# A hierarchical expert stage: the next expert's gate product between up and down, hidden by one activation ahead of the weight splits, and a plain float down product

## The chip, the cores and the metric

The kernel runs on one core of a Trainium2 chip. The metric is the time of one execution on the device, in microseconds. "Before" is the kernel as it stood; its time is the median of three runs.

## The reference

One step of a one-layer streaming encoder over 304 tokens (16 meta tokens, 256 prompt frames, 32 sample frames) with a model width of 2048, all in float32. A projection feeds an RG-LRU branch and an mLSTM branch, their mix is added to x, and then a hierarchical mixture of experts follows. The change lies in the expert part:

```python
def hier_moe(x, w_rg, b_rg, w_re, b_re, w_g, w_u, w_d):
    ...
    gates = jnp.sum(jax.nn.one_hot(eid, N_EXPERTS, dtype=F32) * top_w[..., None], axis=1)
    for e in range(N_EXPERTS):
        hdn = jax.nn.silu(xf @ w_g[e]) * (xf @ w_u[e])
        out = out + gates[:, e:e + 1] * (hdn @ w_d[e]).astype(F32)
```

There are 16 experts in 4 groups, with w_g and w_u of 2048x512 and w_d of 512x2048. A token goes to one group and to the two best experts in it, so most rows of a dense product would be zero; the kernel gathers the rows of each expert instead.

## The kernel before, in words

The kernel is written by hand for five engines, with semaphores. Up to the router it computes products with 128 weight columns at a time; each float weight and activation is split into a rounded high part (fp32r) and the rounded rest, and three rounded products (high by high, high by low, low by high) stand for one float product. The gate products of the RG-LRU (L639) are plain float products, and so are the transposes and the small sums.

The expert stage starts at L814. Tokens are ranked within their expert; an expert has 64 slots per round, and two experts make a pair of 128 rows. The number of rounds is computed on the chip (`nrounds`) and is 1 with these inputs, so the loop over `nr * NPAIR` runs over eight pairs. POOL gathers the 128 rows of a pair into `rows` (L1764, L1766), and TensorE transposes them into banks 0 to 3 (L825). ScalarE writes their rounded part and VectorE the rest into `xs` (L1131, L1627), side by side, so that one product with a stationary tile of 128 columns takes both: rows 0 to 63 of the result belong to the high part, rows 64 to 127 to the rest, and the two halves are added later.

An expert's weights come as six units of 2 MB: two for gate, two for up, two for down. They lie in `ring`, four slots of 2 MB, and SyncE loads unit n+4 into the slot of unit n when TensorE is done with n (`groups_done`, L544). A unit has two halves. ScalarE copies a half, rounded, into one of four buffers `w_high` (L1125), and VectorE overwrites the half in the ring with the rest, `w_low` (L1620).

TensorE takes gate and up of an expert as 16 products each unit (L847 and L848: high and low weights, 512 columns). ScalarE copies the two results into `gu` (L1139), TensorE adds their halves and turns them by products with `add2` (L861), ScalarE takes silu (L1154), and VectorE multiplies by up into `hf`, rounds it and takes its rest (L1646, L1648, L1650). The down product (L878 to L880) has 64 stationary columns, three rounded products for each of 16 tiles, and adds up in banks 0 to 3. VectorE copies them out into `ysb` (L1660), a slice of the tile that the profile names HB, and POOL stores both experts of a pair to `slot_out` (L1775). The transposes of the next pair's rows need the same banks 0 to 3, and stand between up and down of the second expert (L855).

Every engine executes its own list of instructions in order, so the place of a wait in that list decides what stands behind it. The lists in the loop body, before:

- SyncE: the six units of the first expert, then those of the second, in that order, each with its wait.
- TensorE: for each expert gate, gate, up, up, (transposes in the second), adds, down, down.
- ScalarE: splits of the first four units, with the copies of gate and up among them, the split of the first down unit, silu, (row splits), the other down unit and the first unit of the next expert.
- VectorE: rests of four units, the hidden product and its two parts, (rests of rows), rests of the down units, the wait for the down product, the result copies.

In the profile the buffer numbers are left out, `XG` holds `gu`, `sg` and `hf`, and `tri` holds `add2`.

Of the kernel before, what the change touches and what calls it, by code (L numbers as in the profile page):

```python
# [35 lines left out]
def build(nc, A, O):  # L36
# [6 lines left out]
    P = 128  # L43
# [12 lines left out]
    DE = A["w_exp_gate"].shape[3]  # L56
# [40 lines left out]
    with ctx:  # L97
# [80 lines left out]
        nrounds = sb("nrounds", [P, 1], I32)  # L178
# [45 lines left out]
        hs_high = rounded("hs_high", "XG", HALF + UW + 2 * DE + 2 * HC, HC)  # L224
        hs_low = rounded("hs_low", "XG", HALF + UW + 2 * DE + 3 * HC, HC)
# [84 lines left out]

        FIRST = {"xr": 0, "gr": DR, "q": C_Q, "k": C_Q + NH * DQK, "v": C_V, "og": C_OG, "mgr": C_MG}
# [49 lines left out]
        xgt_ready = sem("xgt_ready")  # L361
# [24 lines left out]
        h_steps = sem("h_steps")  # L386
# [85 lines left out]
        def _(sp):  # L472
# [64 lines left out]
            n = sp.value_load(nrounds[0:1, 0:1], min_val=1, max_val=MAXR)  # L537


            def pair(q, turn):  # L540

                for u in range(4, 12):

                    sp.wait_ge(groups_done, turn * 12 + (G_MOE + u - 3))  # L544
                    sp.dma_start(unit_view(u % 4, u % 6), expert_unit(bass.ds(q * 2 + u // 6, 1), u % 6)
                                 ).then_inc(slot_full[u % 4], 16)

            with sp.Fori(0, n * NPAIR - 1) as t:
                pair(t % NPAIR, t)

                for b in range(4):
                    sp.wait_ge(groups_done, t * 12 + (G_MOE + 8 + b + 1))
                    sp.dma_start(unit_view(b, b), expert_unit(bass.ds(((t + 1) % NPAIR) * 2, 1), b)).then_inc(slot_full[b], 16)
            pair(NPAIR - 1, n * NPAIR - 1)

            sp.wait_ge(groups_done, n * (NPAIR * 12) + (G_MOE - 12 + 8 + 1))
            sp.dma_start(unit_view(0, 0), expert_unit(slice(0, 1), 0)).then_inc(slot_full[0], 16)

            for b in range(4):
                wait_apart(sp, rounds_ready, slot_full[b], n * (NPAIR * 3 * 16) + (LOADS_MOE[b] + (1 if b == 0 else 0)) * 16)  # L560
# [3 lines left out]
        def _(pe):  # L564
# [250 lines left out]
            pe.sem_inc(halves_used, 2)  # L815
            pe.wait_ge(rounds_ready, 1)
            nr = pe.value_load(nrounds[0:1, 0:1], min_val=1, max_val=MAXR)
# [10 lines left out]
            gather_transpose(1)  # L828
            with pe.Fori(0, nr * NPAIR) as p:
                for e in range(2):  # L830
                    if e == 0:
                        pe.wait_ge(xgt_ready, p + 1)


                    for u in range(4):
                        ru, c = 6 * e + u, u // 2
                        if u % 2 == 0:

                            pe.wait_ge(gu_copied, p * 4 + (2 * e + c + 1))
                        for f in range(2):  # L840

                            pe.wait_ge(w_rest, p * 24 + (2 * ru + f + 1))
                            w_hi, w_lo = w_high[(2 * ru + f) % 4], half(w_low[ru % 4], f)
                            for k in range(KE):
                                kk = ((u % 2) * 2 + f) * KE + k
                                lhs = xs[:, kk, e, :]
                                pe.matmul(bank[4 + c][:, 0:DE], lhs, w_hi[:, k, :], start=(kk == 0), stop=False)  # L847
                                last = pe.matmul(bank[4 + c][:, 0:DE], lhs, w_lo[:, k, :], start=False, stop=(kk == KD - 1))  # L848
                            if f == 0:
                                last.then_inc(halves_used, 1)  # L850
                        last.then_inc(groups_done, 1)
# [973 lines left out]
```

## Time and profile before

| | |
|---|---|
| median of 3 runs | 2123.28 us (2123.07 to 2130.36) |
| the profiled execution's own time | 2126.67 us |
| its span in the profile | 2125.2 us |
| TensorE busy | 1898.9 us (89%) |
| VectorE busy | 1248.4 us (59%) |
| ScalarE busy | 1001.4 us (47%) |
| moved by DMA | 426.94 MB, mean 201 GB/s |

Busy time of TensorE is modelled from pipelined products, so neighbouring records overlap; how long a product holds the engine is read from the distance between two starts. The clock column of a stretch is the granted TensorE clock as a share of 2.4 GHz; 0.50 is the lower level, 1.2 GHz. Times in the timeline are from the span's start. A releaser in brackets is what ended the engine's idle time.

### The profile page before, as it was taken

How to read it: one execution, taken by the hardware profiler on the slowest of the kernel's cores; microseconds unless marked ns; L12 is line 12 of the kernel's file. 1: busy time of each engine (PE TensorE's matmuls, PEld its weight loads, DVE VectorE, ACT ScalarE, POOL GpSimd, SP SyncE). 2: the span in 40 equal slices, each digit the busy share in tenths (PEclk: the TensorE clock that was granted, in tenths of full speed). 3: DMA queues.
4: the chain of work that ended last, by engine and by line, in shares of the span. 5: the costliest groups of instructions: out<-in, count | busy, mean ns of one | idle time of the engine just before them, and what ended most of it. 6: DMA issues, size and time to landing. Idle time of an engine off the chain costs nothing.

```text
span 2125.2 us, 27688 instructions
## 1 busy us (share of the span) xinstructions
PE 1898.9 (89%) x11579; PEld 1679.6 (79%) x11579; DVE 1248.4 (59%) x1347; ACT 1001.4 (47%) x928; POOL 100.0 (5%) x188
## 2 busy tenths in 40 slices
PE   6999999999999999999999999656888888888860
PEld 5999999999999999999999999644555555556540
DVE  4764553466555556634344544435888888888763
ACT  4334554453344444442333323205767767676741
POOL 3001001000000000000000000010000000000001
PEclk8999999999999999999999999857999989999885
DMA  7655464454444444455566585415899889889854
GB/s 170 159 159 134 128 162 132 117 149 122 127 127 127 127 127 130 129 159 161 155 157 193 155 203 158 189 37 217 346 385 364 350 332 399 347 336 405 326 200 138
DMA packets 379016, 426.94 MB, mean 201 GB/s; under 512 B 13727, under 2 KB 358651, under 8 KB 362265
## 3 DMA queue, kind: packets, MB, share of 16 engines
q1 hardware_dynamic: 369497, 384.24, 55.6%
q0 software_dynamic: 8080, 34.21, 4.7%
q10 hardware_dynamic: 1344, 7.09, 1.2%
q8 instruction: 76, 1.25, 0.3%
q14 instruction: 19, 0.16, 0.0%
HBM read 410.06 MB, written 15.45 MB: 200 GB/s over the span
## 4 chain that ended last, share of the span: by engine, by line
PE 76%; DVE 9%; DMA 8%; issue 4%; ACT 2%; POOL 1%; DVEq 0%; ACTq 0%; POOLq 0%; SPq 0%
PE bank L583 15%; PE bank L585 15%; PE bank L584 15%; DMA ring<-in_w_exp_down 4%; PE bank L878 3%; PE bank L879 3%; DVE w_low L1620 3%; PE bank L880 3%; PE bank L639 3%; PE bank L743 2%; PE bank L745 2%; PE bank L744 2%; PE bank L847 1%; PE bank L848 1%; PE bank L861 1%
## 5 line engine op out<-in xcount | busy, mean ns | idle before, releaser
L1211 DVE TENSOR_TENSOR low<-ring,high 128x2048 fp32r<-128x2048 f32 x172 | 394.1, 2291 | 564.8 <-ACT high L911 564.5
L583 PE MATMUL bank<-x_high,high 128*128 128x304 f32 x2160 | 661.4, 306 | 1.1 <-DVE low L1211 1.1
L585 PE MATMUL bank<-x_high,low 128*128 128x304 f32 x2160 | 652.2, 302 | 0.0
L911 ACT ACTIVATE high<-ring 128x2048 fp32r<-128x2048 f32 x172 | 329.1, 1913 | 543.7 <-DMA ring<-in_w_in 320.9
L584 PE MATMUL bank<-x_low,high 128*128 128x304 f32 x1904 | 572.3, 301 | 0.0
L1620 DVE TENSOR_TENSOR w_low<-ring,w_high 128x2048 fp32r<-128x2048 f32 x194 | 433.5, 2282 | 68.8 <-ACT w_high L1125 67.6
L1125 ACT ACTIVATE w_high<-ring 128x2048 fp32r<-128x2048 f32 x194 | 364.1, 1913 | 144.1 <-PE bank L880 75.9
L583 PEld LDWEIGHTS bank<-x_high,high 128*128 128x128 f32 x2160 | 406.1, 188 | 6.2 <-issue 3.3
L585 PEld LDWEIGHTS bank<-x_high,low 128*128 128x128 f32 x2160 | 406.1, 188 | 0.0
L584 PEld LDWEIGHTS bank<-x_low,high 128*128 128x128 f32 x1904 | 358.6, 188 | 1.4
L847 PE MATMUL bank<-w_high,xs 128*128 128x512 f32 x512 | 212.3, 415 | 27.5 <-DVE w_low L1620 17.6
L848 PE MATMUL bank<-w_low,xs 128*128 128x512 f32 x512 | 202.1, 395 | 0.0
L847 PEld LDWEIGHTS bank<-w_high,xs 128*128 128x128 f32 x512 | 96.9, 189 | 85.6 <-DVE w_low L1620 62.5
L878 PE MATMUL bank<-w_high,hs_high 128*64 128x512 f32 x256 | 114.1, 446 | 49.1 <-DVE xs L1627 34.3
L584 PE MATMUL bank<-hb_rounded,high 128*128 128x304 f32 x512 | 154.8, 302 | 0.0
L879 PE MATMUL bank<-w_high,hs_low 128*64 128x512 f32 x256 | 111.7, 436 | 0.0
L848 PEld LDWEIGHTS bank<-w_low,xs 128*128 128x128 f32 x512 | 97.3, 190 | 18.2
L880 PE MATMUL bank<-w_low,hs_high 128*64 128x512 f32 x256 | 111.2, 434 | 0.0
L878 PEld LDWEIGHTS bank<-w_high,hs_high 128*64 128x64 f32 x256 | 39.2, 153 | 79.4 <-issue 60.9
L584 PEld LDWEIGHTS bank<-hb_rounded,high 128*128 128x128 f32 x512 | 96.2, 188 | 0.0
L583 PE MATMUL bank<-ym_high,high 128*128 128x304 f32 x256 | 77.7, 304 | 0.0
L585 PE MATMUL bank<-ym_high,low 128*128 128x304 f32 x256 | 77.5, 303 | 0.0
(357 smaller groups left out, 2103.5 us busy)
## 6 DMA issues: line engine op xcount, KB each, us to landing
ring<-in_w_in SPq DMA_DIRECT2D x120, 1024.0 KB, 5.6
ring<-in_w_exp_gate SPq DMA_DIRECT2D x33, 2048.0 KB, 10.4
ring<-in_w_exp_up SPq DMA_DIRECT2D x32, 2048.0 KB, 7.4
ring<-in_w_exp_down SPq DMA_DIRECT2D x32, 2048.0 KB, 9.5
ring<-in_w_proj_rnn SPq DMA_DIRECT2D x20, 1024.0 KB, 5.9
ring<-in_w_proj_mlstm SPq DMA_DIRECT2D x16, 1024.0 KB, 5.9
ring<-in_w_out SPq DMA_DIRECT2D x16, 1024.0 KB, 5.9
slot_out<-HB POOLq DMA_DIRECT2D x8, 1024.0 KB, 11.8
```

The source lines that it names most:

```text
L583: pe.matmul(dst, hi[:, k, :], rhs_high(k), start=(k == 0), stop=False)
L584: pe.matmul(dst, hi[:, k, :], rhs_low(k), start=False, stop=False)
L585: last = pe.matmul(dst, lo[:, k, :], rhs_high(k), start=False, stop=(k == KD - 1))
L847: pe.matmul(bank[4 + c][:, 0:DE], lhs, w_hi[:, k, :], start=(kk == 0), stop=False)
L848: last = pe.matmul(bank[4 + c][:, 0:DE], lhs, w_lo[:, k, :], start=False, stop=(kk == KD - 1))
L878: pe.matmul(dst, hh, w_hi[:, b, :], start=(k == 0), stop=False)
L879: pe.matmul(dst, hl, w_hi[:, b, :], start=False, stop=False)
L880: last = pe.matmul(dst, hh, w_lo[:, b, :], start=False, stop=(k == KE - 1))
L911: act.activation(high[n % 4], raw[n % 4], ACT.Copy).then_inc(t_split, 1)
L1125: act.activation(w_high[(2 * ru + c) % 4], half(w_raw[b], c), ACT.Copy).then_inc(w_split, 1)
L1211: v.tensor_tensor(low[n % 4], raw[n % 4], high[n % 4].bitcast(F32), ALU.subtract).then_inc(t_rest, 1)
L1620: v.tensor_tensor(half(w_low[ru % 4], c), half(w_raw[ru % 4], c), w_high[(2 * ru + c) % 4].bitcast(F32), ALU.subtract).then_inc(w_rest, 1)
```

## The change

The down product takes the float weights from the ring as they are loaded, with `hf` as the stationary operand, so down units are neither split nor rounded. The pipeline over experts is shifted: TensorE computes the next expert's first gate unit before the adds of this expert, its second gate unit after them, and then this expert's down. The transposes of the next rows move between the two up units of the second expert. Rows are split expert by expert. Loads follow TensorE's new order. The splits of the very first unit move ahead of the router's exponentials. The last pair is peeled off the loop, so nothing is gathered, transposed or loaded for a pair that doesn't come; `nrounds` gets a second word, the number of pairs less one (`tail`). A function `p(m, c)` gives `tail * m + c` or the loop's register times m, plus c.

```diff
             def unit(t, j, e, k):
+                sp.wait_ge(groups_done, t * 12 + (G_MOE + j - 1))
+                b = (2 + j) % 4
+                sp.dma_start(unit_view(b, k), expert_unit(e, k)).then_inc(slot_full[b], 16)
+            def pair(q, turn, after):
+                first, second = bass.ds(q * 2, 1), bass.ds(q * 2 + 1, 1)
+                unit(turn, 2, second, 0)
+                unit(turn, 3, second, 1)
+                unit(turn, 4, first, 4)
+                unit(turn, 5, first, 5)
+                unit(turn, 6, second, 2)
+                unit(turn, 7, second, 3)
...
+                    unit(turn, 8, after, 0)
+                    unit(turn, 9, after, 1)
+                    unit(turn, 10, second, 4)
+                    unit(turn, 11, second, 5)
+                    unit(turn, 12, after, 2)
+                    unit(turn, 13, after, 3)
...
+            def down(p, s, e):
+                pe.wait_ge(h_act, p(2, e + 2))
+                for u in range(2):
+                    pe.wait_ge(slot_full[(s + u) % 4], p(48, ((s + u) // 4 + LOADS_MOE[0] + 1) * 16))
+                    for c in range(2):
+                        k = 2 * u + c
+                        w = half(w_raw[(s + u) % 4], c)
+                        for b in range(4):
+                            last = pe.matmul(bank[b][0:CAP, 0:DE], hf[:, k * CAP:(k + 1) * CAP], w[:, b, :],
+                                             start=(k == 0), stop=(k == KE - 1))
+                    last.then_inc(groups_done, 1)
+            def pair(p, more):
+                gate_up(p, 2, 2, 0, 2)
+                gate_up(p, 3, 3, 0, 3)
+                pe.wait_ge(gu_copied, p(4, 1))
+                gate_up(p, 4, 4, 1, 0)
+                add_halves(p, 0)
+                gate_up(p, 5, 5, 1, 1)
+                pe.wait_ge(y_out, p(2, 1))
+                down(p, 6, 0)
+                gate_up(p, 8, 6, 1, 2)
+                if more:
+                    pe.wait_ge(y_out, p(2, 2))
+                    gather_transpose(p(1, 2))
+                gate_up(p, 9, 7, 1, 3)
+                if more:
+                    pe.wait_ge(gu_copied, p(4, 3))
+                    pe.wait_ge(xs_ready[0], p(1, 2))
+                    gate_up(p, 10, 8, 0, 0)
+                add_halves(p, 1)
+                if more:
+                    gate_up(p, 11, 9, 0, 1)
+                    pe.wait_ge(xs_ready[1], p(1, 2))
+                    down(p, 12, 1)
+                else:
+                    pe.wait_ge(y_out, p(2, 2))
+                    down(p, 10, 1)
...
             def pair(p, more):
+                split_unit(p, 4, 4)
+                split_half(p, 5, 5, 0)
+                copy_gu(p, 3, 0, 1)
+                split_half(p, 5, 5, 1)
+                silu_of(p, 0)
+                copy_gu(p, 5, 1, 0)
+                split_unit(p, 8, 6)
+                split_unit(p, 9, 7)
+                if more:
+                    split_half(p, 10, 8, 0)
+                    split_rows(p(1, 2), 0)
+                    split_half(p, 10, 8, 1)
+                    split_half(p, 11, 9, 0)
+                copy_gu(p, 9, 1, 1)
+                if more:
+                    split_half(p, 11, 9, 1)
+                    split_rows(p(1, 2), 1)
+                silu_of(p, 1)
+                if more:
+                    copy_gu(p, 11, 0, 0)
+                    split_unit(p, 14, 10)
+                    split_unit(p, 15, 11)
...
+            def hidden(p, e):
+                v.wait_ge(silu_done, p(2, e + 1))
+                v.tensor_tensor(hf, sg, bank[6][:, HC:2 * HC], ALU.mult).then_inc(h_act, 1)
...
+            def pair(p, more):
+                rest_unit(p, 4, 4)
+                rest_unit(p, 5, 5)
+                hidden(p, 0)
+                rest_unit(p, 8, 6)
+                rest_unit(p, 9, 7)
+                results_out(p, 7, 0)
+                if more:
+                    rest_half(p, 10, 8, 0)
+                    rest_of_rows(p, 8, 0)
+                    rest_half(p, 10, 8, 1)
+                    rest_unit(p, 11, 9)
+                    rest_of_rows(p, 8, 1)
+                hidden(p, 1)
+                if more:
+                    rest_unit(p, 14, 10)
+                    rest_unit(p, 15, 11)
+                    results_out(p, 13, 1)
+                else:
+                    results_out(p, 11, 1)
...
```

Units are numbered here in TensorE's order: 2 and 3 are the first expert's up, 4 and 5 the second's gate, 6 and 7 the first's down, 8 and 9 the second's up, 10 and 11 the next pair's gate, 12 and 13 the second's down, 14 and 15 the next pair's up. `gate_up`, `copy_gu`, `add_halves` and `results_out` hold the same instructions as before, and POOL's list is the old one with the last gather left out.

## Rows read from the trace of the kernel before

**Rows 1.** Page, part 4: the chain that ended last, shares by line.

```profile
PE bank L583 15%; PE bank L585 15%; PE bank L584 15%; DMA ring<-in_w_exp_down 4%; PE bank L878 3%; PE bank L879 3%; DVE w_low L1620 3%; PE bank L880 3%; PE bank L639 3%; PE bank L743 2%; PE bank L745 2%; PE bank L744 2%; PE bank L847 1%; PE bank L848 1%; PE bank L861 1%
```

**Rows 2.** Windows: length, busy us of five engines, clock, DMA share, GB/s; whole stage.

```profile
1447.00:2062.10 615.10, 521.41 (x2192) 353.40 (x2192) 507.14 (x340) 435.21 (x292) 18.80 (x23) 0.92 0.85 343
```

**Rows 3.** Chain in order of time: start us, us; first, last transposes; last copies.

```profile
1507.18 1.75 PE bank L825 x16
...
2038.76 1.75 PE bank L825 x16
...
2060.13 1.88 DVE HB L1660 x3
```

**Rows 4.** Timeline of TensorE in one pair: start us, us.

```profile
1657.34 1.91 PE L825 MATMUL bank<-ident,HB 128*128 128x128 f32 x16
...
1665.27 0.68 PE L878 MATMUL bank<-w_high,hs_high 128*64 128x512 f32 x1 [4.29 <-DVE xs L1627]
...
1667.88 0.44 PE L878 MATMUL bank<-w_high,hs_high 128*64 128x512 f32 x1
...
1677.59 0.39 PE L847 MATMUL bank<-w_high,xs 128*128 128x512 f32 x1
...
1680.99 0.39 PE L848 MATMUL bank<-w_low,xs 128*128 128x512 f32 x1
1682.52 0.50 PE L847 MATMUL bank<-w_high,xs 128*128 128x512 f32 x1 [1.14 <-DVE w_low L1620]
...
1699.03 1.97 PE L861 MATMUL bank<-tri,XG 128*128 128x64 f32 x8 [2.55 <-ACT XG L1139]
1702.79 0.68 PE L878 MATMUL bank<-w_high,hs_high 128*64 128x512 f32 x1 [1.79 <-DVE hs_low L1650]
```

**Rows 5.** Page, part 5: weight rests and splits; busy, mean ns, idle before.

```profile
L1620 DVE TENSOR_TENSOR w_low<-ring,w_high 128x2048 fp32r<-128x2048 f32 x194 | 433.5, 2282 | 68.8 <-ACT w_high L1125 67.6
L1125 ACT ACTIVATE w_high<-ring 128x2048 fp32r<-128x2048 f32 x194 | 364.1, 1913 | 144.1 <-PE bank L880 75.9
```

**Rows 6.** Windows of 5 us in one pair, columns as in rows 2.

```profile
1665.00:1670.00 5.00, 4.73 (x16) 2.66 (x17) 4.52 (x3) 2.44 (x3) 0.00 (x0) 0.70 0.15 62
...
1680.00:1685.00 5.00, 3.79 (x16) 2.50 (x15) 5.00 (x4) 3.40 (x2) 0.62 (x1) 1.00 1.02 351
...
1695.00:1700.00 5.00, 2.45 (x16) 2.21 (x14) 3.74 (x2) 4.98 (x4) 0.57 (x1) 0.87 1.01 429
1700.00:1705.00 5.00, 3.21 (x11) 2.01 (x11) 3.64 (x5) 4.24 (x4) 0.99 (x1) 0.50 1.02 436
```

**Rows 7.** Groups by shape: the plain gate products, and the router's products.

```profile
L639 PE MATMUL bank<-XG,HB 128*128 128x307 f32 x208 | 55.7, 421 | 0.0
...
L799 PE MATMUL bank<-wrt,HB 128*128 128x20 f32 x64 | 13.8, 382 | 0.6 <-DVE HB L1543 0.6
```

**Rows 8.** Timeline of TensorE: twenty records of plain gate products in a row.

```profile
179.99 5.33 PE L639 MATMUL bank<-XG,HB 128*128 128x307 f32 x20
```

**Rows 9.** Timeline of TensorE at the start of the stage.

```profile
1447.01 3.68 PE L825 MATMUL bank<-ident,HB 128*128 128x128 f32 x16 [27.61 <-DMA HB<-xn_rows,gidx]
1454.06 0.79 PE L847 MATMUL bank<-w_high,xs 128*128 128x512 f32 x1 [3.38 <-DVE xs L1635]
...
1459.77 0.40 PE L848 MATMUL bank<-w_low,xs 128*128 128x512 f32 x1
```

**Rows 10.** DMA issues at 1672, 1681, 1681 and 1701 us: KB, us to landing.

```profile
ring<-in_w_exp_up SPq DMA_DIRECT2D x1, 2048.0 KB, 7.3
...
ring<-in_w_exp_down SPq DMA_DIRECT2D x1, 2048.0 KB, 12.6
slot_out<-HB POOLq DMA_DIRECT2D x1, 1024.0 KB, 13.1
...
HB<-xn_rows,gidx POOLq DMA_INDIRECT x1, 9.7
```

**Rows 11.** Timeline of VectorE: the result copies of one expert.

```profile
1677.79 2.48 DVE L1660 COPY HB<-bank 64x512 f32<-64x512 f32 x4 [1.28 <-PE bank L880]
```

More of the change, by code:

```diff
@@ L360, in build @@
         rows_t_done = sem("rows_t_done")
-        xgt_ready = sem("xgt_ready")
+        xs_ready = [sem(f"xs_ready{e}") for e in range(2)]
         h_act = sem("h_act")
@@ new lines, in gate_up @@
+            def gate_up(p, s, q, e, u):
+                dst = bank[4 + u // 2][:, 0:DE]
+                for f in range(2):
+                    pe.wait_ge(w_rest, p(16, 2 * q + f + 1))
+                    w_hi, w_lo = w_high[(2 * q + f) % 4], half(w_low[s % 4], f)
+                    for k in range(KE):
+                        kk = ((u % 2) * 2 + f) * KE + k
+                        pe.matmul(dst, xs[:, kk, e, :], w_hi[:, k, :], start=(kk == 0), stop=False)
+                        last = pe.matmul(dst, xs[:, kk, e, :], w_lo[:, k, :], start=False, stop=(kk == KD - 1))
+                    if f == 0:
+                        last.then_inc(halves_used, 1)
+                last.then_inc(groups_done, 1)
@@ L886, in _ @@
+            gather_transpose(1)
+            pe.wait_ge(xs_ready[0], 1)
+            pe.wait_ge(xs_ready[1], 1)
+            gate_up(first, 0, 0, 0, 0)
+            gate_up(first, 1, 1, 0, 1)
+            with pe.Fori(0, tail) as p:
+                pair(lambda m, c: p * m + c, True)
+            pair(lambda m, c: tail * m + c, False)
         @block.scalar
@@ L1161, in _ @@
+            split_unit(first, 1, 1)
+            split_rows(1, 0)
+            split_rows(1, 1)
+            split_unit(first, 2, 2)
+            copy_gu(first, 1, 0, 0)
+            split_unit(first, 3, 3)
+            with act.Fori(0, tail) as p:
+                pair(lambda m, c: p * m + c, True)
+            pair(lambda m, c: tail * m + c, False)
             for i, (t, n) in enumerate(TT):
@@ L1548, in _ @@
             step(v.memset(rk, 0.0))
+            for c in range(2):
+                v.wait_ge(w_split, c + 1)
+                v.tensor_tensor(half(w_low[0], c), half(w_raw[0], c), w_high[c].bitcast(F32), ALU.subtract).then_inc(w_rest, 1)
             v.wait_ge(logits, 1)
@@ new lines, in results_out, with pair @@
+            def results_out(p, s, e):
+                v.wait_ge(groups_done, p(12, G_MOE + s + 1))
+                if e == 0:
+                    v.wait_ge(y_free, p(1, 1))
+                for b in range(4):
+                    last = v.tensor_copy(ysb[0:CAP, e, b * DE:(b + 1) * DE], bank[b][0:CAP, 0:DE])
+                last.then_inc(y_out, 1)
+            def pair(p, more):
+                rest_unit(p, 4, 4)
[15 more added lines that the diff above has]
+                    results_out(p, 13, 1)
+                else:
+                    results_out(p, 11, 1)
@@ L1664, in _ @@
+            rest_unit(first, 1, 1)
+            rest_of_rows(first, 0, 0)
+            rest_of_rows(first, 0, 1)
+            rest_unit(first, 2, 2)
+            rest_unit(first, 3, 3)
+            with v.Fori(0, tail) as p:
+                pair(lambda m, c: p * m + c, True)
+            pair(lambda m, c: tail * m + c, False)
             for i, (t, n) in enumerate(TT):
```

232 lines of the change are left out of this document (79 added, 153 removed).

## The prediction, made before the changed kernel was run

> **What bounds the kernel now.** The chain of waits comes first: its shares by line name TensorE products almost everywhere, with two strangers among the expert lines, the loads of the down weights and the weight rests on VectorE [rows 1]. So the end of the expert stage is set by TensorE, but not by its work alone. The stage runs from the first row transposes at 1447.0 to the end of the last result copies at 2062.0, which is 615.0 us of the 2125.2 us span. In it TensorE counts as busy for 521 us, the granted clock is 0.92 and the transfers have a share of 0.85 [rows 2, 3]. The chain in order of time has the transposes once per pair of experts: eight of them, 1507.18 to 2038.76, so a pair takes 531.6 / 7 = 75.9 us [rows 3].
>
> The timeline of TensorE inside one pair tells where these go. A gate or up unit (16 products) takes 3.6 us at full pace ((1680.99 - 1677.59) / 15 = 0.227 each); a down product of one expert (48) takes 1677.59 - 1665.27 = 12.3 us, of which 2.6 us, to 1667.88, run at half pace; transposes and adds take 1.75 us each. Eight units, two downs without the slow part (11.0 each), one set of transposes and two sets of adds are 29 + 22 + 5.3 = 56.3 us. The other 19.6 us are mostly the waits of 4.29, 2.55, 1.79 and 1.14 us (the last comes once in either expert), 2.6 us for the half pace after two of them, and the twelve halves of units that come at the pace of the VectorE rest (2.28 us) and not at 1.83 [rows 4, 5]. The transfers aren't the bound yet: full stretches move 429 to 436 GB/s, and right after 1665 they nearly stop, since all four ring slots are held [rows 6]. The two queues that would matter next are thus the ring and VectorE.
>
> **The change, part by part.** The down product becomes plain float. Per expert that removes four weight halves from ScalarE (1.91 us) and VectorE (2.28 us) [rows 5], and the cast and low part of hidden from the path to down. It puts 16 plain products in place of 48 rounded ones. What a plain product costs is in the gate products of the RG-LRU, which are plain: 208 records for 104 products, and 20 records of 307 columns begin in (5.33 - 0.42) / 19 = 258 ns each, two clocks per column [rows 7, 8]. 512 columns are then 0.43 us a record and 0.86 us a product; an expert's down takes 13.8 us, 2.8 more than before. Two places of the Trainium skill differ here. In the Trainium skill, "FP8 and Floating Point Precision", TensorE Precision Notes, true FP32 goes through the array four times, which speaks against giving up three rounded products; the trace agrees, with two records of two clocks per column. In the Trainium skill, "Perfetto Trace Analysis", Engine Utilization, FP32_LOW_HIGH halves the output rate; by that alone a down would take 6.9 us, and the two records do not bear it out.
>
> The next expert's gate product goes between up and down, and silu ahead of the splits that wait for weights. The chain adds, silu (0.4), product (0.4) now runs beside a unit of 3.6 us, so of the waits of 4.29, 2.55 and 1.79 us I cost at most 1.3 us per pair. If that unit is late, the chain is late with it and nothing is lost twice.
>
> What is late next follows from the new orders. The ring is four slots in TensorE's own order, and load n+4 is issued when unit n is done. Two down units now hold two slots for 6.9 and 13.8 us, while only two others can load. And on VectorE the result copies of the first expert stand behind both rests of the second expert's second up unit; TensorE's transposes of the next rows wait for these copies, and everything of TensorE stands behind them. That is a new wait with a loop of its own, from transposes to transposes:
> - A, transposes to the end of the second expert's down: transposes 1.75, three units 10.9, adds 1.75, down 13.8 = 28.2 us. TensorE has then idled for some 7 us, and after 27.6 us idle the first transposes took 3.68 us at clock 0.50 [rows 9], while after 4.3 us the half pace lasted 2.6 us of products [rows 4]. I take both, 1.75 + 1.3; the bounds are 0, and 5.7 us of slow products as after the first transposes (1454.06 to 1459.77), 1.55 more. A = 31.2 us.
> - B, from there to the landing of that up unit: its load is the fifth from the one that the end of the down frees. A unit is 2.097 MB, at 430 GB/s 4.9 us, and lands 7.3 us after issue, so 2.4 us are latency [rows 6, 10]. Issue 0.4, latency 2.4, five units 24.5. The store of results and the gather of rows (1.05 MB each) fall into this stretch, since POOL keeps its order. Each costs at least its bytes, 2.4 us. The store costs at most 5.3, by which a load beside it landed later (12.6 against 7.3); I take 4.0, since the rate fell to 351 GB/s there. For the gather, 2.4 to 4.9 (half of its 9.7 us to landing), I take 2.5, since the stretch with it keeps 436 [rows 6, 10]. B = 33.8 us.
> - C, landing to transposes: two halves on ScalarE 3.8, the second rest 2.3, the copies 2.5, and four hand-overs, 0.6 as an estimate [rows 5, 11]. C = 9.2 us.
>
> The sum is 74.3 us against 75.9: the waits are traded for one of 7 to 8 us, plus 5.6 us of extra down.
>
> The two ends of the stage differ. First, weights of units 0 and 1 are split before the rows arrive; the VectorE part lies beside 13.8 us of router products [rows 7]. Rows are split expert by expert, 1.2 us more than the 7.05 us from transposes to first product [rows 9]. From there six units 21.8, half pace 2.9, one wait of 2.1 for a split behind a copy, adds 1.75, down 13.8, a unit 3.6 and 0.5 of hand-overs: 54.7 us, where the old kernel had 60.2. Last, the loop is peeled: no ninth gather, transposes or row split and no spare load. From the last transposes: A 31.2, three units 10.9, adds 1.75, a unit 3.6, waits 1.5, down 13.8, two units with the wait for the last 8.2, copy and adds 3.3, silu and product 1.5, down 13.8, copies 2.9: 92.4 us. Value loads and one VectorE step ahead of the loop are under 0.5 us, and what follows the stage is the same.
>
> 54.7 + 6 x 74.3 + 92.4 = 592.9 us against 615.0: 22 us less. The profiled execution took 2126.67 us, 3.4 over the median of the runs, so I set 2123.28 - 22 = **2101 us**. One microsecond per period is 6 us; break-even lies at a period of 78.0 us. About 0.5%, 10.6 us, is what a measurement of this kernel can tell from no change, which means periods of 76.2 and 79.7 us.
>
> **Rivals.**
> - The new wait doesn't form: POOL's transfers cost their bytes alone and the clock stays up. The period is 74.3 - 1.7 - 3.05 = 69.5 us and the time 2072 us. For it: full stretches beside the gather kept 436 GB/s. Against: the clock fell after each idle of 2.5 us and more [rows 4, 6].
> - It balances out: the half pace lasts 5.7 us of products and the gather takes half of its landing time, +1.55 + 2.4. The period is 78.2 us and the time 2124 us. For it: after the first transposes the pace stayed low for just so long. Against: in the pairs it lasted 2.6 us.
> - Slower: the gather, now in the one stretch where the transfers bound, holds the loads for its whole 9.7 us: +7.2 us, period 81.5, 2144 us. It decides from 6.2 us upward. Before, it ran into a pause of the ring, so its price is hardly shown; the 436 GB/s speak against it.
> - A plain product takes one record at half rate: every down saves 6.9 us, one on each period and on the first stretch and two at the end, so 2101 - 62 = 2039 us. The two records per product speak against it [rows 7]. (It is the reading that the Trainium skill's "Perfetto Trace Analysis", Engine Utilization, would give.)
>
> **How the numbers follow.** Chances: forecast 0.50, no new wait 0.14, balance 0.22, slower 0.12, half rate 0.02. The forecast's own range, 1.7 us either way per period, is 2091 to 2112 us; nine tenths of it are over 0.5% faster. Faster is 0.45 + 0.14 + 0.02 = 0.61, same 0.05 + 0.20 = 0.25, slower 0.12 + 0.02 = 0.14. The range reaches from the no-wait case, 2068, to 2130, and leaves out the slow and the half-rate case and some of the edges.
>
> **What would show it.** Right: 512 plain down records with a pitch of 0.43 us; 128 weight halves on ScalarE where there were 194; no wait of over 1.3 us between adds and down; TensorE idle for 7 to 8 us ahead of each set of transposes, released by VectorE's result copies, with a granted clock near 0.5 behind it; transposes 74 us apart. Wrong: no such idle time, or the copies early and another releaser there; a store or gather that holds the loads for other than 4.0 and 2.5 us; a plain pitch other than 0.43.

## The result, and the profile after

The changed kernel takes 2090.07 us (median of 4 runs, 2085.14 to 2093.76) against 2123.63 us for the kernel before (4 runs): ratio 0.9833, 95% interval 0.9805 to 0.9862 (ratios here and below are taken over all runs and not from the two medians, so they differ slightly from these). The profiled execution took 2093.76 us, with a span of 2092.2 us; like that of before it lies some 3.5 us over its median.

First the window over the expert stage, from the first row transposes to the last result copies, columns as in rows 2:

```profile
1449.70:2029.00 579.30, 525.80 (x1920) 313.10 (x1920) 344.52 (x268) 303.69 (x250) 15.39 (x21) 0.95 0.88 359
```

Against [rows 2] the stage is 35.8 us shorter, while TensorE is busy for 4.4 us more: its idle time fell from 93.7 to 53.5 us. VectorE lost 163 us of work and ScalarE 132 us. The stage begins 2.7 us later, and what follows it takes 63.2 us as before, so the span is 33.0 us shorter.

In the changed kernel L840 are the transposes, L852 and L853 the gate and up products, L864 the adds, L877 the plain down product, L1148 the weight splits, L1683 their rests and L1709 the result copies. The page's chain by line answers to [rows 1]:

```profile
PE bank L598 16%; PE bank L600 15%; PE bank L599 15%; DMA ring<-in_w_exp_up 5%; PE bank L877 5%; PE bank L852 4%; PE bank L853 3%; PE bank L654 3%; DMA ring<-in_w_exp_gate 2%; PE bank L758 2%; PE bank L760 2%; PE bank L759 2%; DVE w_low L1683 2%; ACT w_high L1148 1%; PE bank L840 1%
```

The down weights' loads (4%) are gone from it and the up weights' loads (5%) have come, and the rests on VectorE fell from 3% to 2%. The page's costliest groups name the same engines as [rows 5]:

```profile
L877 PE MATMUL bank<-ring,XG 128*64 128x512 f32 x512 | 224.8, 597 | 1.0 <-DVE XG L1701 1.0
...
L1683 DVE TENSOR_TENSOR w_low<-ring,w_high 128x2048 fp32r<-128x2048 f32 x126 | 283.8, 2287 | 201.7 <-ACT w_high L1148 201.5
...
L1148 ACT ACTIVATE w_high<-ring 128x2048 fp32r<-128x2048 f32 x128 | 240.2, 1915 | 152.5 <-DMA ring<-in_w_exp_up 104.7
...
L840 PE MATMUL bank<-ident,HB 128*128 128x128 f32 x128 | 27.5, 403 | 67.9 <-DVE HB L1709 39.0
```

There are 512 plain down records, and 128 weight splits where there were 194; a split or rest takes as long as before. The line to read is the last one. Transposes waited for nothing in the loop before; now TensorE idles for 39.0 us ahead of them until VectorE's result copies (L1709) are done. The timeline of TensorE shows this once per pair (some rows; start us, us, in brackets the idle time ahead):

```profile
1506.29 1.96 PE L840 MATMUL bank<-ident,HB 128*128 128x128 f32 x16 [1.80 <-DVE HB L1709]
...
1576.77 3.67 PE L840 MATMUL bank<-ident,HB 128*128 128x128 f32 x16 [6.49 <-DVE HB L1709]
...
1648.66 3.67 PE L840 MATMUL bank<-ident,HB 128*128 128x128 f32 x16 [6.48 <-DVE HB L1709]
1651.98 0.71 PE L852 MATMUL bank<-w_high,xs 128*128 128x512 f32 x1
1652.53 0.39 PE L853 MATMUL bank<-w_low,xs 128*128 128x512 f32 x1
...
1659.71 1.89 PE L864 MATMUL bank<-tri,XG 128*128 128x64 f32 x16
...
1665.22 13.95 PE L877 MATMUL bank<-ring,XG 128*64 128x512 f32 x32
...
1935.94 3.53 PE L840 MATMUL bank<-ident,HB 128*128 128x128 f32 x16 [5.90 <-DVE HB L1709]
```

Six periods, 1506.29 to 1935.94, give 71.6 us each, against 75.9 before. No wait stands between adds and down. VectorE in the same period says why the copies are late:

```profile
1707.71 4.49 DVE L1683 TENSOR_TENSOR w_low<-ring,w_high 128x2048 fp32r<-128x2048 f32 x2 [13.54 <-ACT w_high L1148]
1713.23 4.49 DVE L1683 TENSOR_TENSOR w_low<-ring,w_high 128x2048 fp32r<-128x2048 f32 x2 [1.03 <-ACT w_high L1148]
1717.64 2.47 DVE L1709 COPY HB<-bank 64x512 f32<-64x512 f32 x4
```

The copies stand behind the rests of two units. The second pair of rests is unit 9's, whose load ScalarE had awaited until 1711.29. The down product that feeds the copies ended at 1709.91, 7.7 us before they began:

```profile
1695.96 13.95 PE L877 MATMUL bank<-ring,XG 128*64 128x512 f32 x32
```

ScalarE's wait for unit 9, and POOL's list in the same stretch, the store, the index load and the gather:

```profile
1711.29 3.72 ACT L1148 ACTIVATE w_high<-ring 128x2048 fp32r<-128x2048 f32 x2 [1.80 <-DMA ring<-in_w_exp_up]
...
1682.91 0.62 POOL L1855 DMA_DIRECT2D slot_out<-HB  x1 [50.59 <-DVE HB L1709]
1698.17 0.57 POOL L1844 DMA_DIRECT2D gidx<-slot_token  x1 [14.64 <-issue]
1704.49 0.99 POOL L1846 DMA_INDIRECT HB<-xn_rows,gidx  x1 [5.76 <-DMA gidx<-slot_token]
```

The next three windows lie over the transposes of 1648.66, over the idle time ahead of the next pair's transposes, and over the products behind the first. The granted clock is 0.50 over the transposes and 0.72 over the idle time, and the products right behind run at 1.00 again:

```profile
1648.70:1652.40 3.70, 3.70 (x17) 3.70 (x18) 2.02 (x1) 0.03 (x1) 0.00 (x0) 0.50 1.00 425
1715.00:1720.20 5.20, 0.00 (x0) 0.00 (x0) 5.20 (x7) 1.91 (x2) 0.00 (x0) 0.72 0.98 418
1652.40:1665.20 12.80, 12.80 (x64) 10.41 (x63) 9.86 (x12) 8.98 (x13) 0.00 (x0) 1.00 0.76 300
```

### The profile page after: what moved, and what is told of

Its sections match the earlier page's. It is cut to its first block, busy times and chain, and to the rows that moved or that the text cites. A ratio compares the mean times of both kernels' runs of the same rounds, so it can differ in the third digit from the quotient of the medians.

```text
span 2092.2 us, 26760 instructions
## 1 busy us (share of the span) xinstructions
PE 1905.1 (91%) x11307; PEld 1641.0 (78%) x11307; DVE 1090.6 (52%) x1278; ACT 873.4 (42%) x888; POOL 97.1 (5%) x186
## 4 chain that ended last, share of the span: by engine, by line
PE 77%; DMA 10%; DVE 6%; ACT 3%; issue 2%; POOL 1%; DVEq 0%; ACTq 0%; POOLq 0%; SPq 0%
PE bank L598 16%; PE bank L600 15%; PE bank L599 15%; DMA ring<-in_w_exp_up 5%; PE bank L877 5%; PE bank L852 4%; PE bank L853 3%; PE bank L654 3%; DMA ring<-in_w_exp_gate 2%; PE bank L758 2%; PE bank L760 2%; PE bank L759 2%; DVE w_low L1683 2%; ACT w_high L1148 1%; PE bank L840 1%
## 5 line engine op out<-in xcount | busy, mean ns | idle before, releaser
L1683 DVE TENSOR_TENSOR w_low<-ring,w_high 128x2048 fp32r<-128x2048 f32 x126 | 283.8, 2287 | 201.7 <-ACT w_high L1148 201.5
L1148 ACT ACTIVATE w_high<-ring 128x2048 fp32r<-128x2048 f32 x128 | 240.2, 1915 | 152.5 <-DMA ring<-in_w_exp_up 104.7
L877 PE MATMUL bank<-ring,XG 128*64 128x512 f32 x512 | 224.8, 597 | 1.0 <-DVE XG L1701 1.0
L852 PE MATMUL bank<-w_high,xs 128*128 128x512 f32 x512 | 208.3, 407 | 8.8 <-issue 3.9
L853 PE MATMUL bank<-w_low,xs 128*128 128x512 f32 x512 | 201.0, 393 | 0.0
L877 PEld LDWEIGHTS bank<-ring,XG 128*64 128x64 f32 x512 | 69.2, 138 | 148.0 <-issue 147.3
L852 PEld LDWEIGHTS bank<-w_high,xs 128*128 128x128 f32 x512 | 97.6, 191 | 50.2 <-DVE w_low L1683 22.9
L853 PEld LDWEIGHTS bank<-w_low,xs 128*128 128x128 f32 x512 | 97.4, 190 | 18.5
L840 PE MATMUL bank<-ident,HB 128*128 128x128 f32 x128 | 27.5, 403 | 67.9 <-DVE HB L1709 39.0
L840 PEld LDWEIGHTS bank<-ident,HB 128*128 128x128 f32 x128 | 24.6, 215 | 71.0 <-issue 42.0
## 6 DMA issues: line engine op xcount, KB each, us to landing
ring<-in_w_exp_down SPq DMA_DIRECT2D x32, 2048.0 KB, 12.2
```

What stands on the lines that cost most here:

```text
L840: last = pe.transpose(bank[b][:, c * P:(c + 1) * P], rows[:, k * P:(k + 1) * P], ident[:, :])
L852: pe.matmul(dst, xs[:, kk, e, :], w_hi[:, k, :], start=(kk == 0), stop=False)
L853: last = pe.matmul(dst, xs[:, kk, e, :], w_lo[:, k, :], start=False, stop=(kk == KD - 1))
L877: last = pe.matmul(bank[b][0:CAP, 0:DE], hf[:, k * CAP:(k + 1) * CAP], w[:, b, :], start=(k == 0), stop=(k == KE - 1))
L1148: act.activation(w_high[(2 * q + c) % 4], half(w_raw[s % 4], c), ACT.Copy).then_inc(w_split, 1)
L1683: v.tensor_tensor(half(w_low[s % 4], c), half(w_raw[s % 4], c), w_high[(2 * q + c) % 4].bitcast(F32), ALU.subtract).then_inc(w_rest, 1)
```

## The experiments

Theory: the new wait is the copies' place in VectorE's list, and the gain comes from the order, in which silu's place is essential; the plain product alone gains nothing. Each period below is the mean of the six between the second and the eighth set of transposes, unless the text says otherwise. Two profiles of the changed kernel give 71.6 and 71.4 us, two of the order alone 69.6 and 69.7, so a tenth or two of a microsecond tells nothing. Lines with `<-` and three numbers at the end are waits: who waited for whom, us in total, times, longest.

**The copies ahead of the rests.** On VectorE, in the changed kernel:

```diff
                 rest_unit(p, 8, 6)
-                rest_unit(p, 9, 7)
                 results_out(p, 7, 0)
+                rest_unit(p, 9, 7)
```

> Edit: in the changed kernel, VectorE's result copies of the first expert stand ahead of the rests of unit 9 (the second expert's second up unit) and no longer behind them. Theory (the new wait sets the period): TensorE's idle time of 5.6 to 6.9 us ahead of the transposes goes; the copies (2.5 us) and the transposes (1.75, and 1.6 more at half clock) leave the loop, which then runs from the landing of unit 9 through its split and rest straight to its product. Period 71.6 - 5 = 66 to 67 us, with the 12 loads and POOL's two transfers as the next bound (about 64 us); time 2090 - 6 x 5 = about 2060 us. Rival (unit 9 itself is late, and the copies only fill its waiting time): the transposes move ahead, TensorE waits as long for unit 9, period over 70 us, time within 10 us of 2090.

Measured: 2077.26 us (5 runs), ratio 0.9766 (0.9753 to 0.978), period 68.9 us. The wait for the copies is gone and is worth 2.7 us a period, less than expected: the result lies between the theory and the rival. Ahead of some transposes a new releaser stands in its place, in TensorE's timeline and in POOL's:

```profile
1641.40 1.97 PE L840 MATMUL bank<-ident,HB 128*128 128x128 f32 x16 [2.44 <-DMA HB<-xn_rows,gidx]
...
1709.74 1.97 PE L840 MATMUL bank<-ident,HB 128*128 128x128 f32 x16 [3.38 <-DMA HB<-xn_rows,gidx]
```

```profile
1675.55 0.62 POOL L1855 DMA_DIRECT2D slot_out<-HB  x1 [45.36 <-DVE HB L1709]
1690.73 0.57 POOL L1844 DMA_DIRECT2D gidx<-slot_token  x1 [14.56 <-issue]
1697.17 0.99 POOL L1846 DMA_INDIRECT HB<-xn_rows,gidx  x1 [5.88 <-DMA gidx<-slot_token]
```

POOL's list is serial: the store of a pair's results, a wait of 14.6 us until it has landed, the index load, another 5.9 us, and only then the gather of the next rows. In the six periods TensorE waits for it four times, for 7.0 us in all, so it accounts for only part of what was expected and did not come; the transfers' share over them is 0.97. The transposes have also become quick: behind 2.44 and 3.38 us of idle time they take 1.97 us, not 3.67.

**The plain product alone.** The kernel before, in its own order, with the down product taken plain:

```diff
-                                pe.matmul(dst, hh, w_hi[:, b, :], start=(k == 0), stop=False)
-                                pe.matmul(dst, hl, w_hi[:, b, :], start=False, stop=False)
-                                last = pe.matmul(dst, hh, w_lo[:, b, :], start=False, stop=(k == KE - 1))
...
+                                last = pe.matmul(bank[b][0:CAP, 0:DE], hf[:, k * CAP:(k + 1) * CAP], w[:, b, :],
+                                                 start=(k == 0), stop=(k == KE - 1))
...
-                v.tensor_copy(hs_high, hf).then_inc(h_steps, 1)
...
-                    rest_of_weights(p, 6 * e + 5)
```

> Edit: the kernel before, with its order of units, transposes, loads and silu, and only the down product taken as plain float from the ring (no splits or rests of down units, no rounding of hidden). Theory (the gain is in the order): each down takes 2.8 us longer on TensorE and holds its ring slots that much longer, the splits it saves lie beside other work, and the waits between adds and down stay but for the 0.7 us of rounding; period 75.9 us within 1.5 us, time 2115 to 2132 us. Rival (the gain comes from the lighter ScalarE and VectorE): with a third of their splits gone the period falls to 72 us and the time to 2090 to 2105 us.

Measured: 2134.84 us (5 runs), ratio 1.0041 (1.0027 to 1.0054); 9.2 us slower than the 2125.68 us beside it and 3 us above the theory's range; the rival is out. The period is 76.8 us (seven, 1507.49 to 2045.15). Of TensorE's waits in the loop, the one ahead of the down product for the split rows is still there:

```profile
PE bank L877 <- DVE xs L1625: 25.6, 7, 3.7
```

**Silu late.** In the changed kernel, on ScalarE:

```diff
                 split_half(p, 5, 5, 1)
-                silu_of(p, 0)
                 copy_gu(p, 5, 1, 0)
                 split_unit(p, 8, 6)
+                silu_of(p, 0)
                 split_unit(p, 9, 7)
```

> Edit: in the changed kernel, ScalarE's silu of the first expert stands behind the splits of unit 8 (the second expert's first up unit), so it waits for that unit's load. Theory: unit 8 lands 11 to 13 us after silu's sums are ready, so down starts some 15 us later; the end of down, not the landing of unit 9, then releases the copies and the transposes, so the period rises by about 6 to 10 us, to 78 to 82 us, and the time to 2130 to 2150 us. Rival (the place of silu is of no account, since the loop hangs on unit 9): period within 2 us of 71.6, time within 12 us of 2090.

Measured: 2171.09 us (one run), period 80.7 us. The sign is right. The price, 9.1 us a period, is at the upper end, and the time is 21 us over the expected range, because the two ends pay too: the first stretch takes 68.1 us and not 56.6, the tail 105.5 and not 93.0. Silu waits for a load, TensorE waits for silu's product, and while it waits it frees no ring slot:

```profile
PE bank L877 <- DVE XG L1701: 90.0, 6, 16.0
```

So with silu behind these splits, and the gate product in the same new place, the changed kernel is 45 us slower than the kernel before.

**Half of the down product.** The changed kernel with only the first half of each down unit multiplied; the other half of the product is left out:

```diff
-                    for c in range(2):
+                    for c in range(1):
...
-                                             start=(k == 0), stop=(k == KE - 1))
+                                             start=(k == 0), stop=(k == KE - 2))
```

> Edit: the changed kernel with half of the down product left out (the first of two halves of every down unit alone), so a down takes 6.9 us and not 13.8. Theory (the loop from transposes over the second expert's down to the load that it frees): 6.9 us go from each period, which then meets the bound of the transfers, 64 to 66 us; time 2090 - 6 x 6 - 7 - 14 = about 2033 us. Rival (the ring and the transfers already set the period): period 70 us or more, gain at the two ends alone, time 2065 us or more.

Measured: 2068.91 us (one run), period 69.3 us. Of the 14 us that TensorE no longer works per period, 2.3 come back, far from the theory; the time is the rival's, the period 0.7 us below it. The transposes wait here for the gather too, for up to 6.7 us:

```profile
1709.19 3.67 PE L840 MATMUL bank<-ident,HB 128*128 128x128 f32 x16 [6.66 <-DMA HB<-xn_rows,gidx]
```

That made a second theory: POOL's serial list, not the transfers themselves, is the next bound. It needs the gather alone moved, and with the other edits:

```diff
             def store(p, more):
                 if more:
-                    pool.wait_ge(rows_gathered, (p + 1) * 16)
-                    pool.wait_ge(rows_t_done, p + 1)
-                    gather(p + 1, p + 2)
+                    pool.wait_ge(rows_gathered, (p + 2) * 16)
+                    pool.wait_ge(rows_t_done, p + 2)
+                    gather(p + 2, p + 3)
...
             gather(0, 1)
+            pool.wait_ge(rows_gathered, 16)
+            pool.wait_ge(rows_t_done, 1)
+            gather(1, 2)
...
```

**Early copies and early gather** (the label best):

> The early copies of copies_early, and besides on POOL's list the gather of each pair's rows goes out as soon as the pair before it has been transposed, ahead of the wait for the store, one round early (so there is one gather more in all, of rows that nobody reads). Theory: in copies_early and in half_down the transposes wait for a gather that is late because POOL's list is serial: store, its landing (12.6 to 14.6 us), index, its landing (6 us), gather, its landing (14 us). With the gather out some 45 us earlier its wait goes, and the period falls from 68.9 to what the transfers set: 24 MB of weights, a store and a gather, 27.3 MB in all, at the 418 GB/s of the busiest rows is 65.2 us. So 65.2 to 67.5 for the period, 2055 to 2070 for the run. Rival: copies_early moved 394 GB/s at a DMA share of .96, so the transfers set its period already and the wait for the gather is only where that shows: 68.3 or more, within 5 us of 2077.

Measured: 2067.08 us (5 runs), ratio 0.9728 (0.9713 to 0.9743), period 67.5 us, at the upper end of the theory's range and 0.8 below the rival's. No transposes in the loop wait for anything. Over the six periods TensorE idles for 20 us, where it idled for 39 in the changed kernel, and the transfers reach a share of 0.98:

```profile
1503.49:1908.69 405.20, 385.13 (x1442) 225.19 (x1440) 262.15 (x205) 234.21 (x193) 33.37 (x18) 1.00 0.98 404
```

**The early gather alone.** The changed kernel with POOL's edit only:

> The changed kernel with the early gather alone; the result copies stay behind the rests of unit 9. Theory: there the transposes are released by the result copies, and the gather's own time no longer lies in front of the load of unit 9, so the gather is worth little: period 71.6 within 1, time 2084 to 2094. Rival: the gather still takes its 2.5 us out of the stretch from the second expert's first up product to unit 9's landing: period 69.1 or less, 2076 or less.

Measured: 2086.16 us (5 runs), ratio 0.981 (0.9795 to 0.9825), period 70.4 us. The time is in the theory's range, the period at its lower edge: 1.2 us a period lie between the theory's 0 and the rival's 2.5. In time alone the gain isn't clear, since the interval overlaps the changed kernel's. The copies still release the transposes, after 3.9 to 5.1 us of idle time instead of 5.6 to 6.9.

**A second store.** That kernel, with each pair's results stored twice:

```diff
                 pool.dma_start(slot_out[bass.ds(p * P, P), :].rearrange("(e s) n -> s e n", e=2), ysb[0:CAP]).then_inc(y_stored, 16)
-                pool.wait_ge(y_stored, (p + 1) * 16)
+                pool.dma_start(slot_copy[bass.ds(p * P, P), :].rearrange("(e s) n -> s e n", e=2), ysb[0:CAP]).then_inc(y_stored, 16)
+                pool.wait_ge(y_stored, (p + 1) * 32)
```

> gather_early, with each pair's results stored a second time into a place that nobody reads, right behind the first store. Theory: a store lies in the stretch in which the loads wait for nothing but the transfers, so it costs what its megabyte takes of them, the term of the prediction (4.0, between 2.4 and 5.3): the period is 2.4 to 5.3 longer than that of gather_early, and the time 16 to 37 us longer. Rival: the transfers have room by then, the store is hidden: period within 0.8, time within 6.

Measured: 2106.95 us (one run), period 73.0 us, 2.6 more than without it, at the lower end of the theory's range: a store costs nearly its bytes there and no more (1.05 MB in 2.6 us is 403 GB/s).

**Half of the down product, early gather.** Half of the product is left out as above:

> half_down (half of the down product left out) with the early gather. Theory: half_down's gain was held back by the gather, on which its transposes waited 5.4 to 6.9 us; without that wait its period falls from 69.3 to between 64.5 and 66.5, the time to between 2043 and 2055. Rival: the transfers (391 GB/s in half_down) are at their limit: period 68 or more, 2060 or more.

Measured: 2062.59 us (one run), period 68.5 us: the rival's numbers came. The gather's wait of up to 6.7 us is gone, but the transposes now wait for the copies, and TensorE waits for weight rests as it did before (54.8 us between 1560 and 1990 us, 49.3 in the kernel without the early gather):

```profile
PE bank L852 <- DVE w_low L1683: 54.8, 24, 4.0
PE bank L840 <- DVE HB L1709: 24.3, 6, 4.2
```

The rival's reason isn't shown by this: over the six periods the transfers' share is 0.94 here, while the kernel with early copies and gather, with all of the down product, has 0.98 and a shorter period. Half of the product with both early moves wasn't tried.

**The order alone.** The changed order, with the down product in rounded pieces as before. Each slot has its two splits and rests again, those of the first down behind silu 0, those of the second behind silu 1:

```diff
                 silu_of(p, 0)
+                split_unit(p, 6, 6)
                 copy_gu(p, 5, 1, 0)
+                split_unit(p, 7, 7)
                 split_unit(p, 8, 6)
...
                 silu_of(p, 1)
...
                 if more:
+                    split_unit(p, 12, 12)
                     copy_gu(p, 11, 0, 0)
+                    split_unit(p, 13, 13)
...
-                            last = pe.matmul(bank[b][0:CAP, 0:DE], hf[:, k * CAP:(k + 1) * CAP], w[:, b, :],
-                                             start=(k == 0), stop=(k == KE - 1))
+                            dst = bank[b][0:CAP, 0:DE]
+                            pe.matmul(dst, hh, w_hi[:, b, :], start=(k == 0), stop=False)
+                            pe.matmul(dst, hl, w_hi[:, b, :], start=False, stop=False)
+                            last = pe.matmul(dst, hh, w_lo[:, b, :], start=False, stop=(k == KE - 1))
```

> The changed order (next pair's gate between up and down, silu ahead of the splits) with the down product in rounded pieces as before: its units are split on ScalarE (the first expert's two behind the silu, the second's two behind the silu of theirs) and get their rests on VectorE, and TensorE makes 48 rounded products in place of 32 plain ones. TensorE has some 3 us less to do for each down product than with the plain one, VectorE some 20 us more and ScalarE some 15 us more per pair, both as in the kernel before. Theory: the order makes the gain by itself, and taking the splits away only gives the rest of it: the period is between 70.5 and 74.5, the time between 2082 and 2112. Rival: without the plain product the order is worth nothing, because the product waits again for its splits and rests, which stand behind the loads on both lists: 75.5 or more, 2115 or more.

Measured: 2080.95 us (5 runs), ratio 0.9802 (0.9789 to 0.9816), period 69.6 us: a little better than the theory's range, and better than the whole change. The splits that came back are mostly covered. The largest of TensorE's waits in the loop is the gather's, ahead of the transposes (here L843); then come those for weight rests, ahead of down (L883) and of gate and up (L855). The lines reach from 1507 to 2030 us and so over the last pair; in the six periods alone the two are 12.7 and 9.9 us, none over 1.6:

```profile
PE bank L843 <- DMA HB<-xn_rows,gidx: 33.6, 6, 7.0
PE bank L883 <- DVE w_low L1699: 19.5, 15, 4.6
PE bank L855 <- DVE w_low L1699: 12.5, 8, 1.6
```

**The order with early copies and early gather:**

> order_alone with the early result copies and the early gather of the best kernel so far (2067 us, period 67.5, DMA share .96). Theory: that kernel stands at the transfers, so the 6 us that TensorE saves per pair are worth little, and the 20 us more on VectorE and 15 us more on ScalarE delay the pieces for which TensorE waits: period 67 to 71, time 2063 to 2090, no faster than the kernel with the plain product. Rival: that kernel's period is still set in part by TensorE's 30.5 us stretch ahead of the second expert's up product, and the shorter products take it to 66 or less, 2057 or less.

Measured: 2058.85 us (5 runs), ratio 0.9696 (0.9682 to 0.9709), period 66.5 us. It falls between the two expectations, but the theory's "no faster" is out: it is the fastest kernel of the study, 0.3% under the same kernel with the plain product (each against the kernel before on its own chip), and their intervals don't overlap. The transfers are busy for 0.99 of the loop, while TensorE idles for 42 us of it:

```profile
1502.01:1900.98 398.97, 356.64 (x1633) 252.82 (x1632) 377.23 (x277) 320.61 (x240) 38.37 (x18) 0.99 0.99 410
```

**Plain or rounded, on one chip.** The changed kernel and the order alone once more, unchanged and side by side, since their intervals overlapped:

> The changed kernel once more, on one chip and against the same runs of the kernel before as the next one, because their two intervals so far ([0.9805, 0.9862] and [0.9789, 0.9816]) overlap. Theory: the plain product costs in the new order what it cost in the old one, 9 us: the changed kernel stands between 2086 and 2094, and 6 to 12 us behind the one with the rounded product. Rival: the two are equal, within 3 us, and the difference was that of the chips.

> order_alone once more, beside the changed kernel on one chip. Theory: between 2078 and 2084, 6 to 12 us ahead of the changed kernel. Rival: within 3 us of it.

Measured: 2089.58 us, ratio 0.9848 (0.9821 to 0.9875), and 2081.11 us, ratio 0.9802 (0.9784 to 0.9821), 5 runs each. The theory holds: 8.5 us lie between the medians, and although the intervals meet at 0.9821, each of the five runs with the rounded product is faster than all five with the plain one.

| down product | old order | new order | new order, early copies and gather |
|---|---|---|---|
| rounded | 2123.6 us, period 75.9 | 2081.0, 69.6 | 2058.9, 66.5 |
| plain | 2134.8, 76.8 | 2090.1, 71.6 | 2067.1, 67.5 |

The times are from several chips, on which the kernel before took 2122.3 to 2125.7 us. "New order" stands for everything in the change besides the plain product. That includes the peeled last pair, the row splits expert by expert and the early splits of the first unit, which weren't tried one by one.

## Why the prediction was right

The direction, the range and the mechanism were right; the forecast of 2101 us was 11 us too slow, 1 us outside the forecast's own 2091 to 2112, and three terms were mis-sized: the slow products in A, the gather and the store in B.

- **Plain product.** 32 records take 13.95 us, a pitch of 0.44 us, where 0.43 and 13.8 us were forecast. With 512 records for 256 products the half-rate rival is out.
- **Adds, silu and product off the path.** No wait ahead of down is over 1.0 us, as forecast, but the text gave it as a matter of course. The late silu shows that this hangs on one line's place: 9.1 us a period.
- **The new wait.** Forecast: 7 to 8 us of idle time, released by the result copies behind unit 9's rests, clock near 0.5 behind it. Measured: 5.6 to 6.9 us, that releaser, clock 0.50. Moving the copies took it away, so the cause is shown.
- **A, 31.2 us.** It took 30.5 us (1648.66 to the end of down at 1679.17). Of the two terms for the clock, the slow transposes came (3.67 us for 1.75), and the slow products, 1.3 us, did not: the first product behind them took 0.71 us and the next 0.39. The 1.3 us came from [rows 4], where products met the slow clock right after an idle time; here the transposes met it first.
- **B, 33.8 us.** It took 32.1 us (to 1711.3). This is the larger miss. In it the gather had 2.5 us and the store 4.0 us. POOL issued the gather only at 1704.49, 25.3 us into the stretch, because it waited 14.6 us for the store and 5.8 us for the index, so most of its transfer fell behind unit 9's load (0.43 of its 1.05 MB moved before 1711.3); moving it elsewhere gave back 1.2 us. A second store cost 2.6 us. With 1.2 and 2.6 B would be 31.1; the last 1.0 us I can't assign, since a second store need not cost what the first does.
- **C, 9.2 us.** It took 9.0 us.
- **The sum.** For that period 71.6 us against 74.3, and six times 2.7 is 16.2 us. The ends gave some of it back: the first stretch took 56.6 us and not 54.7, where the wait for the copies shows as well, with 1.80 us; the tail took 93.0 and not 92.4. So the stage took 579.2 us where 592.9 was forecast. It also began 2.7 us later, so part of the closeness to 2101 is luck: misses of opposite sign.
- **Ahead of the loop.** "Under 0.5 us" was too little. The first transposes begin at 1447.57 to 1449.74 in the twelve profiles with the new order (median 1448.4) and at 1447.01 and 1446.71 in the two with the old one: 0.6 to 3 us. Some 1.0 us of it belongs to the change: from POOL's first instruction behind the router to the index load it is 14.2 us in the changed kernel and 13.2 before. POOL's issue gap ahead of the index load, where its second value load stands, grew from 2.69 to 3.27 us, and one issue before it from 2.30 to 2.75; what causes the latter is open, and neither was tried alone. The rest was there already at 1379 us, when POOL stores the rows, and differs as much between two profiles of the changed kernel (1380.46 and 1379.08).

The prediction also held against "no new wait" that the clock fell after each idle of 2.5 us and more. That is not so throughout: behind 2.44 and 3.38 us it stayed at 1.00 in the kernel with early copies.

Of the rivals, "no new wait" was wrong, since the wait came. That its period of 69.5 us lies near the 68.9 of the early copies is chance, for its sum still has the copies in C. "Balance" and "slower" gave the gather a price of 4.9 and 9.7 us; the 1.2 us is against both. What no rival held is the result of the last column and the last line of the table: the plain product, half of this change by its title, costs some 9 us in either order. The prediction had its 2.8 us per down on the path as the price of the change, and did not ask what the order would give without it. The order with the rounded product takes the split work back and is faster all the same: VectorE's extra 19 us a pair mostly find room beside the loads (379 of 418 us busy in six periods, and TensorE waits there 33.6 us for the gather and 22.6 us for weight rests).

## What to carry to other kernels

When a product is moved to hide a chain, look at each engine's list for the one small step that now stands behind a transfer: silu's place was worth 9 us a period, the copies' place 2.7, the gather's 1.2 to 1.4. A change of two parts is to be tried part by part; here one part gained 41 us and the other lost 9, and the sum hid it. A share of the transfers of 0.98 doesn't yet mean that only fewer bytes help: the same kernel with the shorter down product gained 1.0 us a period with the same bytes, at a share of 0.99. What fewer bytes would give wasn't tried.

## What the runs showed of the hardware that was not expected

The index load moves 0.5 KB, and its time goes with what else is under way. In the changed kernel POOL waited 5.76 us for it beside full transfers; in the kernel with half of the down product and the early gather, 2.51 us, in a stretch in which the ring had all but stopped. The two windows, with DMA share and GB/s at the end, first of the changed kernel:

```profile
1698.10:1704.50 6.40, 6.40 (x16) 2.06 (x15) 0.00 (x0) 0.00 (x0) 0.57 (x2) 1.00 1.03 440
```

and of the other:

```profile
1578.50:1581.70 3.20, 3.20 (x15) 2.63 (x15) 1.98 (x5) 3.20 (x4) 0.64 (x2) 1.00 0.03 10
```

Both occur in one kernel, the one with the early gather alone: POOL waited 6.44 us for its first index load in the loop, at a share of 1.00, and 2.49 to 2.57 us for the other five, at 0.02 to 0.21. The first two:

```profile
1508.75:1515.75 7.00, 7.00 (x33) 5.51 (x31) 5.77 (x7) 7.00 (x8) 0.56 (x1) 1.00 1.00 391
1578.88:1582.04 3.16, 3.16 (x15) 2.63 (x14) 1.95 (x5) 3.16 (x4) 0.59 (x2) 0.98 0.07 26
```

So in the changed kernel a list that waits for store, index and gather in turn takes over 30 us (14.6, 5.8 and 12.2 us), small as the index is.

Less work on TensorE came with a lower granted clock: 0.89 between 1560 and 1990 with half of the down product, where TensorE idled for 4.0 to 6.7 us ahead of each set of transposes and the whole sets took 3.67 us. With early copies and gather it doesn't idle there; the clock is 1.00 over six periods, and the sets take 1.91 to 1.96 us. The length of the idle time alone doesn't decide it: one set took 1.97 us behind 3.38 us of idle time (early copies) and another 3.67 us behind 3.25 us (the order alone). Their windows, in this order:

```profile
1709.74:1711.70 1.96, 1.96 (x17) 1.96 (x18) 1.21 (x1) 1.70 (x1) 0.00 (x0) 1.00 0.98 418
1505.22:1508.90 3.68, 3.68 (x17) 3.68 (x18) 2.07 (x1) 0.00 (x0) 0.00 (x0) 0.50 1.00 427
```
